# Six input panels of a streaming-encoder trunk by seven half-size products, with the normed rows parked in memory and a new order of ranks inside a block

## The reference, cut to what matters

```python
h = layer_norm(x, ln0_g, ln0_b)
proj = h @ w_in            # 1024 x 5640: p (512), u (1024), v (1024), o (1024), i/f gates (8), branch gates (2048)
y_pool = pool_mixer(p) @ w_branch_pool
uc = silu(causal_depthwise_conv(u));  q, k = uc @ w_q, uc @ w_k
h_out = sigmoid(o) * group_norm(mlstm(q, k, v, i, f))
mix = (sigmoid(g0) * y_pool + sigmoid(g1) * (h_out @ w_branch_mlstm)) @ w_out
h = layer_norm(alpha * h + mix)
ffn = sum over the token's 4 of 32 experts of gate * (swiglu(h @ w_e1[e] + b_e1[e]) @ w_e2[e] + b_e2[e])
out = layer_norm(alpha * h + ffn)
```

## Time and profile before

| what | value |
|---|---|
| median of 3 runs | 1601.42 us (1600.19 to 1601.58) |
| the profiled execution, own time | 1602.21 us |
| its span, first to last instruction | 1600.2 us |
| TensorE busy | 1438.3 us (90%) |
| VectorE, ScalarE, GpSimd busy | 634.0, 151.7, 324.7 us |
| moved by DMA | 474.15 MB, 296 GB/s over the span |
| chain that ended last | TensorE 67%, DMA 21%, issue 7%, VectorE 3% |

### The profile page before, as it was taken

How to read it: one execution, slowest core, us unless ns; L and a number is a source line. 1 busy time by engine, 2 the same in 40 slices (tenths; PEclk the granted TensorE clock), 3 DMA queues, 4 the chain that set the end, 5 groups by cost and what they waited for, 6 DMA issues and landing times.

```text
span 1600.2 us, 29384 instructions
## 1 busy us (share of the span) xinstructions
PE 1438.3 (90%) x12182; PEld 678.4 (42%) x12183; DVE 634.0 (40%) x1124; ACT 151.7 (9%) x263; POOL 324.7 (20%) x384
## 2 busy tenths in 40 slices
PE   7999999999999997799982988898789899999986
PEld 6744444456664643234331333233233333435332
DVE  5024344332223763543531554344334433434455
ACT  4011332211110111000000000000000000000001
POOL 1060000000000032332330433223323322323210
PEclk9999999999999999899997999999999999999999
DMA  5522200162316279999999899999999999999986
GB/s 190 175 70 78 72 0 1 46 197 60 79 46 276 103 270 421 423 421 423 422 417 394 323 421 421 423 424 421 422 422 425 419 424 424 425 398 418 424 371 264
DMA packets 99209, 474.15 MB, mean 296 GB/s; under 512 B 18036, under 2 KB 63868, under 8 KB 74216
## 3 DMA queue, kind: packets, MB, share of 16 engines
q1 hardware_dynamic: 82592, 453.48, 70.2%
q0 software_dynamic: 12080, 16.64, 2.9%
q10 hardware_dynamic: 4504, 3.57, 0.7%
HBM read 469.08 MB, written 20.99 MB: 306 GB/s over the span
## 4 chain that ended last, share of the span: by engine, by line
PE 67%; DMA 21%; issue 7%; DVE 3%; ACT 1%; POOL 0%; SPq 0%; POOLq 0%; DVEq 0%
PE ps L1772 23%; DMA big<-in_w_e 20%; PE ps L1798 12%; PE ps L1509 5%; PE ps L1586 5%; PE ps L1470 4%; PE ps L1648 3%; PE ps L1676 3%; PE ps L1632 3%; PE ps L1616 2%; PE ps L1626 2%; PE ps L1537 1%; PE ps L1555 1%; DMA big<-expert_rows 1%; PE ps L1693 0%
## 5 line engine op out<-in xcount | busy, mean ns | idle before, releaser
L1772 PE MATMUL ps<-big,rest 128*32 128x512 f32 x5024 | 567.0, 603 | 102.4 <-DMA big<-in_w_e 42.7
L1772 PEld LDWEIGHTS ps<-big,rest 128*32 128x32 f32 x5024 | 170.1, 111 | 485.6 <-issue 475.4
L1798 PE MATMUL ps<-big,rest 128*32 128x256 f32 x5120 | 294.0, 380 | 22.0 <-DMA big<-in_w_e 18.6
L1798 PEld LDWEIGHTS ps<-big,rest 128*32 128x32 f32 x5120 | 175.3, 110 | 150.3 <-issue 43.1
L1323 DVE MEMSET stat<- 128x1 f32 x30 | 1.8, 59 | 426.2 <-PE ps L1772 426.2
L691 POOL DMA_INDIRECT rest<-x_rows,idx x120 | 147.5, 1229 | 57.2 <-issue 31.7
L712 POOL DMA_INDIRECT expert_rows<-rest,slot x124 | 123.4, 995 | 55.7 <-issue 29.3
L916 ACT ACTIVATE rest<-rest 128x1024 f32<-128x1024 f32 x32 | 33.9, 1061 | 916.0 <-DVE rest L1302 701.2
L699 POOL COPY idx<-P 128x4 uint32 (+1 forms) x30 | 5.6, 186 | 467.4 <-DVE rest L1324 458.8
L1509 PE MATMUL ps<-big,rest 128*128 128x512 f32 x192 | 84.4, 602 | 2.8 <-ACT big L772 2.8
L673 POOL IOTA P<- 128x128 f32 x1 | 0.2, 244 | 374.6 <-DVE rest L1170 374.6
(11 more groups left out here) (293 smaller groups left out, 1144.3 us busy)
## 6 DMA issues: line engine op xcount, KB each, us to landing
big<-in_w_e SPq DMA_DIRECT2D x189, 2048.0 KB, 25.9
rest<-in_w_in SPq DMA_DIRECT2D x14, 1024.0 KB, 5.2
big<-expert_rows SPq DMA_DIRECT2D x4, 2048.0 KB, 16.2
gate_area<-in_w_in SPq DMA_DIRECT2D x8, 512.0 KB, 5.4
rest<-in_w_in SPq DMA_DIRECT2D x8, 512.0 KB, 4.7
big<-in_w_out SPq DMA_DIRECT2D x1, 4096.0 KB, 13.5
X<-in_x SPq DMA_DIRECT2D x4, 512.0 KB, 9.6
gate_area<-in_w_branch_mlstm SPq DMA_DIRECT2D x4, 512.0 KB, 6.3
```

The costliest lines, as they stand in the source:

```text
L1772: last = mm(ps[TB * g:TB * (g + 1), h0 + b, :], rows[:, k, b, :], w1, start=(k == 0), stop=(k == end))
L1798: last = mm(ps[TB * g:TB * (g + 1), 4 + b // 2, YW * (b % 2):YW * (b % 2 + 1)], acts[:, k, b, :], rows[:, k, YW * g:YW * (g + 1)], start=( ...
```

## The change

The six input panels are computed by the same seven half-size products as the gates: `seven_products` takes the weights, the banks and a running number `q` (0 to 5 for the panels, 6 to 11 for the gates). The 128x128 quarters of a panel are cut out of its ring slot. The two columns of a panel are thus made together, the early half of the second by ScalarE's last copy, the rest by VectorE (`sum_halves`). The banks are 4 or 0 in turn for the running sum, and 5, 6, 7. The sums of the input must exist before the first panel, so `mix_rows` moves ahead and puts them into the columns of `X0`; the residual there is stored to memory when it is ready, and read back when the eighth gate group's products are done. Both transfers are in SyncE's queue, the store ahead of the fifth panel's load, and it takes over the wait that stood further down. The first `seven_products` wait for single weight sums, and the seventh product no longer waits for the sixth; `mix_w_used` is gone. GpSimd's pooling takes its temporaries from `wtmp`. Lastly two more iotas (in `head_sel`) replace `iota_row` for `pick` and `at_place`: position 4s + q of a block holds rank s + 8q, so that neighbouring ranks are 4 partitions apart.

```diff
-        mix_h = [cut(big, V_AT + HK * HALF * n, HK, HALF) for n in range(4)]
+        mix_h = [cut(X0, HK * HALF * n, HK, HALF) for n in range(4)]
+        N_WIDE = PW // PANEL + MW // PANEL
+        WIDE_BANKS = [(4, 5, 6, 7), (0, 5, 6, 7)]
+        GATE_BANKS = (2, 3, 6, 7)
...
+                if n == H - 1:
+                    sp.wait_ge(h0_ready, NT)
+                    sp.dma_start(h0_dram.rearrange("(i p) d -> p i d", p=P), X0v).then_inc(h0_stored, 16)
                 if n == 5:
-                    sp.wait_ge(h0_ready, NT)
...
+            sp.wait_ge(h0_stored, 16)
+            sp.wait_ge(gate_done, KD)
+            sp.dma_start(X0v, h0_dram.rearrange("(i p) d -> p i d", p=P)).then_inc(h0_back, 16)
             sp.wait_ge(merged_ready, KD)
...
-                pool.wait_ge(gemm_out, at[("p", g)] + 1)
+                if g % 2 == 0:
+                    pool.wait_ge(top_done, g + 2)
+                else:
+                    pool.wait_ge(halves_summed, g // 2 + 1)
+                    pool.wait_ge(gemm_out, at[("p", g)] + 1)
...
+            step(nc.gpsimd.iota(rank_row.rearrange("p (b s q) -> p b s q", b=NB, s=TS), pattern=[[TB, NB], [1, TS], [TS, TQ]], ...
+            step(nc.gpsimd.iota(place_row.rearrange("p (s q b) -> p s q b", b=NB, s=TS), pattern=[[NB, TS], [NB * TS, TQ], [1, NB]], ...
...
+            def copy_halves(q, banks):
+                for n in range(3):
+                    act.wait_ge(sum_done, 3 * q + n + 1)
+                    if n == 0 and q >= 1:
+                        act.wait_ge(halves_summed, q)
+                    act.activation(part[n], ps[:, banks[0], 0:HALF], ACT.Copy).then_inc(sum_copied, 1)
+            def take_wide(q, n, dst):
+                banks = WIDE_BANKS[q % 2]
+                copy_halves(q, banks)
+                act.wait_ge(gemm_done, n + 1)
+                act.activation(dst, ps[:, banks[0], 0:HALF], ACT.Copy).then_inc(gemm_out, 2)
...
-            for c in range(MC):
-                take(("u", c), uT[:, c, CPAD:CPAD + S])
-                if c >= 1:
-                    silu(c - 1)
+            for c in range(1, MC, 2):
+                take_wide((PG + c) // 2, at[("u", c)], uT[:, c, CPAD:CPAD + HALF])
+                if c >= 3:
+                    silu(c - 3)
+                    silu(c - 2)
+            silu(MC - 2)
             silu(MC - 1)
...
+            def mix_rows():
+                dve.wait_ge(h0T_ready, KD * NT)
+                dve.wait_ge(h0_stored, 16)
...
+            def mix_weights(q, landed, count, w):
+                w11, w12, w21, w22 = w
+                dve.wait_ge(landed, count)
+                if q >= 1:
+                    dve.wait_ge(part_done, 3 * q)
+                nc.vector.tensor_tensor(mix_w[0], w21, w22, ALU.add).then_inc(mix_w_ready, 1)
+                dve.wait_ge(mix_w_ready, 4 * q + 1)
+                nc.vector.tensor_tensor(mix_w[1], mix_w[0], w11, ALU.subtract).then_inc(mix_w_ready, 1)
+                nc.vector.tensor_tensor(mix_w[2], w11, w21, ALU.subtract).then_inc(mix_w_ready, 1)
+                dve.wait_ge(mix_w_ready, 4 * q + 2)
+                nc.vector.tensor_tensor(mix_w[3], w12, mix_w[1], ALU.subtract).then_inc(mix_w_ready, 1)
...
+            mix_rows()
+            mix_panel(0)
+            sum_panel(0, pT, 0, PAD)
+            mix_panel(1)
             dve.wait_ge(if_done, 2)
...
+            for q in range(1, PG // 2):
+                sum_panel(q, pT, 2 * q, PAD)
+                mix_panel(q + 1)
             for c in range(MC):
-                dve.wait_ge(gemm_out, at[("u", c)] + 1)
+                q = (PG + c) // 2
+                if c % 2 == 0:
+                    sum_panel(q, uT, c, CPAD)
+                    if q + 1 < N_WIDE:
+                        mix_panel(q + 1)
+                    dve.wait_ge(top_done, 2 * q + 2)
+                else:
+                    dve.wait_ge(halves_summed, q + 1)
+                    dve.wait_ge(gemm_out, at[("u", c)] + 1)
...
-                nc.vector.tensor_scalar(pick[:, i, :], iota_row, 1.0, ...
+                nc.vector.tensor_scalar(pick[:, i, :], rank_row, 1.0, ...
-                    nc.vector.tensor_scalar(at_place, iota_row, place[:, n:n + 1], ...
+                    nc.vector.tensor_scalar(at_place, place_row, place[:, n:n + 1], ...
             def layer_norm_1(i):
+                if i == 0:
+                    dve.wait_ge(h0_back, 16)
...
+            def seven_products(q, w, banks):
+                if q >= 1:
+                    pe.wait_ge(halves_summed, q)
+                product(banks[0], w11, h0_first[:, :, 0:HALF], True).then_inc(sum_done, 1)
+                pe.wait_ge(mix_h_ready, 1)
+                pe.wait_ge(mix_w_ready, 4 * q + 1)
+                product(banks[2], mix_w[0], mix_h[0], True).then_inc(part_done, 1)
+                pe.wait_ge(mix_h_ready, 2)
+                pe.wait_ge(mix_w_ready, 4 * q + 2)
+                pe.wait_ge(sum_copied, done + 1)
+                product(banks[0], mix_w[1], mix_h[1], False).then_inc(sum_done, 1)
+                product(banks[1], w12, h0_second[:, :, 0:HALF], True).then_inc(part_done, 1)
+                pe.wait_ge(mix_h_ready, 4)
+                pe.wait_ge(mix_w_ready, 4 * q + 4)
+                pe.wait_ge(sum_copied, done + 2)
+                product(banks[0], mix_w[2], mix_h[2], False).then_inc(sum_done, 1)
+                product(banks[3], mix_w[3], h0_second[:, :, HALF:S], True).then_inc(part_done, 1)
+                pe.wait_ge(sum_copied, done + 3)
+                return product(banks[0], w22, mix_h[3], False)
...
-                for c in range(2):
-                    b = bank_for(n_out)
-                    for k in range(KD):
-                        last = mm(ps[:, b, :], slot[:, k, P * c:P * (c + 1)], h0T[:, k, :], ...
-                    last.then_inc(gemm_done, 1)
-                    n_out += 1
+                pe.wait_ge(gemm_out, max(n_out - 2, H * NT - 1))
+                seven_products(n - H, quarters(ring[:, n % RING], True), WIDE_BANKS[(n - H) % 2]).then_inc(gemm_done, 2)
+                n_out += 2
...
+                    pe.wait_ge(halves_summed, N_WIDE)
+                    pe.wait_ge(gemm_out, n_out)
                     pe.wait_ge(wpool_landed, 16)
```

More of the change, by code:

```diff
@@ L198, in build_program, with quarters @@
         part_sum = hn[:, 3 * HALF:4 * HALF]
-        SUM_BANK, PART_BANK, TAIL_BANK, REST_BANK = 2, 3, 6, 7
+        N_WIDE = PW // PANEL + MW // PANEL
+        WIDE_BANKS = [(4, 5, 6, 7), (0, 5, 6, 7)]
+        GATE_BANKS = (2, 3, 6, 7)
+        def quarters(w, row):
+            return [w[:, HK * k:HK * (k + 1), P * c:P * (c + 1)] for c in range(2) for k in range(2)] if row else [w[:, HK * n:HK * (n + 1), :] for n in range(4)]
         sig_o = [gate_area[:, MERGE_ROWS * P:MERGE_ROWS * P + S], big[:, SIG_O_AT:SIG_O_AT + S]]
@@ L817, in _ @@
             act.activation(t0_row, t0_row, ACT.Ln, bias=1.0).then_inc(log_ready, 1)
-            for g in range(PG):
-                take(("p", g), pT[:, g, PAD:PST])
+            for q in range(1, PG // 2):
+                take_wide(q, at[("p", 2 * q + 1)], pT[:, 2 * q + 1, PAD:PAD + HALF])
             act.wait_ge(tot_ready, 1)
@@ L873, in _ @@
             for m in range(2, KD):
-                for n in range(3):
-                    act.wait_ge(sum_done, 3 * (m - 2) + n + 1)
-                    act.activation(part[n], ps[:, SUM_BANK, 0:HALF], ACT.Copy).then_inc(sum_copied, 1)
+                copy_halves(N_WIDE + m - 2, GATE_BANKS)
                 act.wait_ge(gate_done, m + 1)
@@ L1123, in _ @@
             head_out(H - 1)
[L1126 to L1144, removed]
@@ L1471, in v_product, with product @@
                 last.then_inc(gemm_done, 1)
+            def seven_products(q, w, banks):
+                w11, w12, w21, w22 = w
+                done = 3 * q
+                def product(b, rows, acts, first):
+                    for k in range(HK):
+                        last = mm(ps[:, b, 0:HALF], rows[:, k, :], acts[:, k, :], start=(first and k == 0), stop=(k == HK - 1), skip_group_check=True)
+                    return last
+                if q >= 1:
[16 more added lines that the diff above has]
+                return product(banks[0], w22, mix_h[3], False)
             def gate_rows():
@@ L1574, in head_tr @@
                     last.then_inc(gemm_done, 1)
-            def seven_products(m):
-                w = merge_w[m % 2]
-                w11, w12, w21, w22 = (w[:, HK * n:HK * (n + 1), :] for n in range(4))
-                done = 3 * (m - 2)
-                def product(b, rows, acts, first):
-                    for k in range(HK):
-                        last = mm(ps[:, b, 0:HALF], rows[:, k, :], acts[:, k, :], start=(first and k == 0), stop=(k == HK - 1), skip_group_check=True)
-                    return last
-                pe.wait_ge(merge_landed[m % 2], 64 * (m // 2 + 1))
-                pe.wait_ge(gate_ready, m)
```

(15 more changed lines are left out.)

80 lines of the change are left out of this document (52 added, 28 removed).

## The result

The changed kernel takes 1579.94 us (median of 4 runs, 1576.63 to 1581.41) against 1601.42 (4 runs, 1600.19 to 1601.58): the ratio is 0.9863, with a 95% interval of 0.9847 to 0.9879. The forecast was 1580.0. The profiled execution took 1579.55 us, its span is 1577.8 where the span before is 1600.2.

The account below looks back on a forecast made before the run. TensorE bounds the panels ahead of the loop, the weight stream the loop. Terms -9.8 - 2.8 - 1.9 + 0.4 - 3.3 - 4.0 = -21.4 us gave 1580.8 profiled, 1580.0 median; range 1572.0 to 1589.0.

Parts of the forecast that it names:

- Products: Six input panels: 56 records in 12.09 us replace 32 in 13.73 us per panel, -9.8 us.
- hole: After the gate rows: TensorE's wait for ScalarE's copy of the first panel's second column goes, -2.8 us.
- clock: Panels behind the gate rows: without the idle gap the granted clock should not fall, -1.9 us.
- new waits: Input panels: TensorE waiting for VectorE, ScalarE and its last copy, +0.4 us; bounds 0 and 1.8 a panel.
- VectorE in the panels: Input panels: VectorE's additions, weight sums and convolution take 10.1 us per panel against TensorE's 12.1.
- rival that VectorE bounds the panels: Input panels: GpSimd's pooling slows VectorE's round to 13.9 us; total between 1583.6 and 1590.8, 1587; chance 0.14.
- The sums of the input and the round trip: Ahead of the panels: early input sums, residual stored and read back, cost nothing; up to 5 us if cover goes.
- The gates: Gate groups: -1.27 us in group 2 and 6 x 0.34 us from removing the sixth-product wait, together -3.3 us.
- wait for the sixth product: Gate groups: removing this wait ahead of the seventh product saves 0.34 us each, 2.0 us in six groups.
- The ranks: Expert loop: spreading empty gather positions evens out DMA engines, -4 us; bounds 0 and 11.6 us.
- two lags: Expert loop: slowest engine's lag of about 2 us won back at the passage to TensorE's bound and at the end.
- rival that the ranks give all: Expert loop: the fullest engine sets every landing, 11.6 us in place of 4.0, total 1572.4; chance 0.10.

Follow-up runs that it names:

- g1: Kernel before the change, plus first-panel copies ahead of the gate rows, the gates' new waits and the new rank order, no half-size panel products: 1583.47 us, ratio 0.9917.
- g4: The changed kernel run again unaltered, as control of its group of runs: 1577.14 us, ratio 0.9868.
- f2: Kernel before the change, with ScalarE copying the first panel's two columns ahead of the gate-row activations: 1596.48 us, ratio 0.9976.
- f1: Kernel before the change, with the new order of ranks alone: 1594.93 us, ratio 0.9963.
- f3: Kernel before the change, with single weight sums waited for and no wait for the sixth product, in the six gate groups alone: 1598.09 us, ratio 0.9985.
- g2: Changed kernel with eight extra VectorE operations of 128x512 behind the weight sums of each of the four u panels: 1592.34 us.
- g3: Changed kernel with the residual's load from memory queued behind the wait for the merge: 1576.16 us.
- f4: Changed kernel with the wait for the sixth product put back ahead of the seventh in all twelve uses: 1583.13 us, ratio 0.9887.
- e1: The changed kernel run again unaltered, as control: 1576.05 us, ratio 0.9857.
- e2: Changed kernel with the ranks in natural order: 1581.78 us, ratio 0.9895.
- e3: Changed kernel with neighbouring ranks 2 positions apart in place of 4: 1578.04 us.
- e4: Changed kernel with neighbouring ranks 8 positions apart in place of 4: 1578.18 us.

## Why the prediction was right, and where it was off

The time came out at 1579.94 for 1580.0 forecast, and the sum of the stages at -22.4 for -21.4. The steps:

- **Products, hole, clock, new waits** (-9.8, -2.8, -1.9, +0.4: -14.1): measured -14.2. The six panels take 12.09 + 60.77 = 72.86 us where six times 12.09 are 72.54, so the waits cost 0.3. The products are shown by themselves, 84.01 to 74.27 us between g1 and g4, 9.7 us; the hole with the clock by f2, 4.5 us in the trace for 4.7. The clock's term was nearly right for the profiled execution (1.65 us against f2's 68.86; the forecast had set it against 68.65) and is not a constant: with the same hole it was 3.1 us in f1 and nothing in f3.
- **VectorE in the panels**: 10.1 us a round forecast, 9.6 measured, and g2 shows that its slack ends within the 5.8 us that were added to a round. The rival that VectorE bounds the panels is out. GpSimd's pooling slowed it, as far as the overlap in time tells: weight sums beside the pooling took up to 1.52 us in place of 0.69, but only in the first three panels, and the rounds there still ended in time.
- **The sums of the input and the round trip**: at no cost, as said. The store took 7.5 us, near the lower bound of 7 and not the 14 that I worked with; the load 7.9. g3 shows more cover than the forecast had seen: it had put a late load at up to 5 us, and 12 us late it cost nothing.
- **The gates**: -3.3 forecast, -3.3 in the trace of the changed kernel and of f3. The wait for the sixth product was put at 0.34 us; f4 has 0.39.
- **The ranks**: this is the term that was mis-sized. The prediction had "such a lag back twice, where the loop passes from the stream's bound to TensorE's and at the end: -4 us". The direction held and the size did not: e1 to e2 and f1 show 5.7 and 5.8 us. The picture of two lags did not hold either. Nothing is won up to the restart, where the forecast had the first lag, and behind it the loss of the natural order grows from landing to landing (2.0, 4.0, 6.4 us in e2) instead of coming back at the end. It is the same whether an expert that TensorE bounds takes 31.6 to 31.9 us (e2) or 32.6 (before): the rest takes 718 us in both, and 712 with 4 apart, at 31.4 us (e1) as at 32.6. That fits an engine whose work sets the pace all the way behind the restart, which is nearer to the rival that the ranks give all; it is an inference, since no row names an engine. The rival's 11.6 us was too high: the fullest group is not full in all blocks, the new order leaves an excess too, and the first eight experts lie ahead of the restart.
- **The size of the ranks' term, as an estimate**: counted on the reference's routing, from the ninth expert on the fullest group of four positions holds 50 rows over the mean in natural order, 28 with 8 apart, 21 with 2 apart and 10 with 4 apart. (The 118, 54, 26 and 70 in the expectations of e3 and e4 are for all experts and count each row twice, once for each of the two quarters that one engine would carry.) If two engines share a group's rows, each has 2 KB of a row to gather and 2 KB to scatter. At 46.4 us for an engine's 1.04 MB that is 0.18 us a row, and by this estimate natural to 4 apart should give 7.1 us (5.8 measured), to 8 apart 3.9 (3.4), to 2 apart 5.2 (2.5). The first two fit roughly; 2 apart fits badly and stays open, on one profile.
- **What hid the size**: the stretch ahead of the restart was 1.2 us longer in the changed profile, and the fifth stretch scatters by 5 us, so the total agreed better than its parts. A part of the agreement to 0.1 us is luck: the control runs gave 20.9 to 23.1 us.

The Trainium skill (DMA: Bandwidth & Descriptors, The descriptor swizzle) says that, in a transfer to 128 partitions, an engine takes groups of four consecutive partitions. The results with natural order, 4 and 8 apart (718.0, 712.2 and 714.6 us) agree with that, the 715.5 us with 2 apart only in direction; no row names an engine, so it was not seen directly, and no other grouping was worked out against it.

## What to carry to other kernels

A DMA share of 0.99 does not mean that nothing is left to win in a stream: look at which positions of gathered rows are always filled, and try spreading the empty ones over the positions; here that gave 5.7 and 5.8 us. Half-size products gave their share of matmuls in their stage (9.7 us of 9.8) because VectorE's whole round fits inside a panel, so write down that round before, and move what the sums need (here the residual's columns) to where a transfer has cover. TensorE's wait for its own last product cost 0.39 us each time; ask whether another wait already implies it.

## What the hardware showed that I had not expected

- Behind the same hole of 2.8 us the clock does not always fall: 160 records took 70.51 us before, 71.97 in f1 and 68.91 in f3, where they took 68.86 without the hole, in f2.
- Experts with three blocks took 32.5 to 32.6 us in some profiles and 31.4 to 31.9 in others, whatever the kernel. In the changed kernel the chain of waits has, between an expert's second and the next one's first product,

```profile
1339.62 10.70 PE ps L1868 x192
1350.33 1.10 issue
1351.42 20.81 PE ps L1842 x192
```

and in e1

```profile
1335.10 10.36 PE ps L1868 x192
1345.46 0.27 issue
1345.72 20.81 PE ps L1842 x192
```

  Most of the difference is in "issue", where nothing shown was waited for. It was the same within each group of runs; what makes it was not tried. It did not change the time from the restart to the end.
- A VectorE addition of two operands of 128x512 took 1.43 to 1.52 us beside GpSimd's pooling (96.44 to 100.79 in the changed kernel), and 0.69 without it.
